# Two 1024 x 1024 branch products in seven half-size products each, their weight sums made in DRAM

## Chip, cores, metric

The kernel runs on one core of a Trainium2 chip. The metric is the device time of one execution in microseconds. Its five engines are TensorE (PE in the profile: matmuls, and weight loads as PEld), VectorE (DVE), ScalarE (ACT), GpSimd (POOL) and SyncE (SP, which here only issues transfers). Each works through its own list in order; semaphores order them against each other.

## What is computed

Two transformer blocks over 512 tokens of width 1024, all in float32. The change lies in the mixing part of the second block:

```python
a = gmlp_spatial_gating(z_u, z_v, ...)         # 512 x 1024
b = forgetting_attention(q, k, v, f_logit, b_f) # 512 x 1024
y_a = a @ w_branch_a                            # 1024 x 1024 weights
y_b = b @ w_branch_b
merged = gate_a * y_a + gate_b * y_b
x = x + merged @ w_out
```

## The kernel before

Activations lie transposed in SBUF: feature on the partition, eight tiles of 128 features by 512 tokens. A float32 product is made of three products of rounded parts: hi x hi, hi x lo and lo x hi. So each operand is split before use: ScalarE writes the high part (a copy into an fp32r tile), VectorE the low part (raw minus high). Weights come as strips of 1 MB (128 x 2048: 256 output features by the whole contraction). A strip has one of three slots: SyncE loads it into w_raw (line 590, after the slot's last product), ScalarE copies it to w_hi (L1375), VectorE writes w_lo over w_raw (L1951). The numbers of the phases (`PHASES`, `FIRST`) fix the order of all strips; `unit_done` counts two units a strip.

`stream` (with `feature_k`, L767 to L769) makes a plain product: 4 strips, 2 units each, a unit being 8 x 3 matmuls of 512 tokens into one PSUM bank, four banks in turn. Some feed-forward products are made instead in seven products of half size (`seven`, L1189 to L1191: Strassen's scheme in Winograd's form), there with tokens as output partitions and weights as the moving operand; their weight sums come from GpSimd's accumulating transfers (`part_sums`, L714) and VectorE.

The order around the change: attention 2a, woven with the product zv; the product u; the products qk2b and v2b; attention 2b woven with gate_b; gate_a; branch_b (operand: the attention, in att_t, split to b_hi and b_lo); branch_a (operand: the gated gMLP, in u_t, split to a_hi and a_lo); out2 (operand: merged); then the up product. VectorE multiplies branch_b's result into merged (L2626), branch_a's into gate_t (L2634), adds the two (L2636) and splits (L2638; ScalarE L1815). In out2 it adds to x (L2030). x waits in DRAM (x_kept) during attention 2b, whose buffers lie in its place, and is loaded back by SyncE (L613) at gate_a's last strip. In the attentions GpSimd stages operands (L667) and normalises score tiles (L674) that TensorE then transposes (L985); VectorE inverts the sums (L2105).

Of the kernel before, what the change touches and what calls it, by code (L numbers as in the profile page):

```python
# [13 lines left out]
P = 128  # L14
D = 1024
# [59 lines left out]
PHASES += [("branch_b", 4), ("branch_a", 4), ("out2", 4)]  # L75
# [9 lines left out]
STRIP_AT = {s: n for n, s in enumerate(s for s in range(N_STRIPS) if s not in MADE)}  # L85


def raw_count(s):

    return 16 * sum(n not in MADE and n not in SPARE for n in range(s, 0, -W_SLOTS))  # L90
# [4 lines left out]
FILLS = {name: 2 * n for name, n in PHASES} | {"wo_att": 8, "ple": 8} | {name: 2 * len(ADDED) for name in SEVEN}  # L95
# [67 lines left out]
def build(nc, d, out):  # L163
    ctx = ExitStack()
    with ctx:
# [139 lines left out]

        up_pad = [sb(f"up_pad{j}", [P, CONV2 - 1 + T], at=work + 2048 + 520 * j) for j in range(4)]
# [104 lines left out]
        m_hi = sem("m_hi")  # L411
        m_lo = sem("m_lo")
# [10 lines left out]
        amix_hi = sem("amix_hi")  # L423
        amix_lo = sem("amix_lo")
# [32 lines left out]
        pool_out_ready, POOL_OUT0 = seg_done, SPARE0 + 32 * len(SEVEN)  # L457

# [41 lines left out]
        def summed_count(g, i):  # L500

            return 16 * (4 * g + list(A_STAGE).index(i) + 1)

        def part_of(part, g):
            k, n = part
            return d["parts"][4 * g + 2 * n + k]

# [24 lines left out]
        def _(sp_eng):  # L532
# [50 lines left out]
            for s in range(1, N_STRIPS):  # L583
                j = s % W_SLOTS
                if s in MADE or s in SPARE:
                    continue
                if s >= W_SLOTS:

                    sp_eng.wait_ge(unit_done, 2 * (s - W_SLOTS) + 2)
                sp_eng.dma_start(w_raw[j].rearrange("p k n -> p (k n)"), d["strips"][STRIP_AT[s]]).then_inc(raw_loaded[j], 16)  # L590
                if s in PARTS_AT:
                    first_parts(PARTS_AT.index(s))
# [17 lines left out]
                if s == FIRST["gate_a"] + 3:  # L610

                    sp_eng.wait_ge(pv_done, 2 * 3 * HEADS8)
                    sp_eng.dma_start(x, x_kept).then_inc(x_loaded[0], 16)  # L613
# [12 lines left out]
        def _(pool):  # L626
# [23 lines left out]
            def attention(call, qk_phase):  # L650
# [37 lines left out]
                for n in range(TILES + 1):  # L688
                    if n and not causal:
                        normalize(n - 1)  # L690
                    if n < TILES - TT:
                        for part in ((0, 1), (2, 3, 4) if causal else (2, 3), (), ())[n % TT]:
                            stage(n // TT + 1, part)
                    if causal and n and n % 2 == 0:

                        normalize(n - 2)
                        normalize(n - 1)

# [9 lines left out]

# [17 lines left out]
            attention("2a", "qk2a")  # L726
            attention("2b", "qk2b")
            for g in range(FF_SEVEN, len(SEVEN)):
# [9 lines left out]
        def _(pe):  # L738
# [538 lines left out]
            stream("branch_b", feature_k, B, ready=lambda k: pe.wait_ge(att_lo, 4 + k + 1))  # L1277
            stream("branch_a", feature_k, A, ready=wait_tiles(amix_lo))
# [1626 lines left out]
```

## Time and profile before

| | |
|---|---|
| median of three runs | 1606.87 us (1606.82 to 1606.89) |
| the profiled execution | 1607.59 us |
| its span | 1605.9 us |
| TensorE busy | 1587.6 us, 99% |
| VectorE, ScalarE, GpSimd busy | 67%, 44%, 11% |
| branch_b starts, up product starts | 1052.45, about 1183 us |

The span runs from the first instruction to the last, the time has some 1.7 us more around it. A matmul's duration overlaps its neighbours', so the distance between starts is what one costs. In a group of instructions the columns are the count, busy time and mean ns of one, and the idle time of the engine before them with what ended it.

### The profile page before, as it was taken

Reading aid. Unit: us, or ns where it says so; the run is one execution under the profiler, and the core shown is the slowest. Engines: PE = TensorE matmul, PEld = TensorE weight load, DVE = VectorE, ACT = ScalarE, POOL = GpSimd, SP = SyncE. Lnnn points to the kernel's source line nnn. Section 1 sums busy time; section 2 is a strip of 40 time slices with the busy share of each in tenths; the row PEclk is TensorE's granted clock in tenths of the full one; section 3 lists DMA queues with packets and bytes.
Section 4 is the critical chain, followed back from the end, with each engine's and each line's share of the span. In section 5 each row is a group of like instructions: output and inputs, shape, how many; then the busy total and the mean of one; then the engine's idle time right before and its main releaser. Section 6 shows DMA issues by size and latency. Waiting matters only on the chain.

```text
span 1605.9 us, 20446 instructions
## 1 busy us (share of the span) xinstructions
PE 1587.6 (99%) x8187; PEld 1305.8 (81%) x8187; DVE 1078.5 (67%) x1494; ACT 710.6 (44%) x1018; POOL 181.5 (11%) x263
## 2 busy tenths in 40 slices
PE   9999999999999999999999999999999999999998
PEld 7877777888888888878788887888888888888888
DVE  6756788669393865657744477445566876878857
ACT  6524575545252524415662156342334443443544
POOL 0001055000000000024500255000000000000000
PEclk9999999999999999999999999999999999999999
DMA  5233321264757522331022211322237347344221
GB/s 191 80 106 125 123 95 53 79 210 131 236 132 235 131 106 94 116 138 72 27 105 83 101 53 53 136 101 105 93 143 262 102 135 238 93 154 158 105 106 53
DMA packets 32894, 195.14 MB, mean 122 GB/s; under 512 B 4320, under 2 KB 6816, under 8 KB 11296
## 3 DMA queue, kind: packets, MB, share of 16 engines
q1 hardware_dynamic: 25056, 160.20, 27.0%
q0 software_dynamic: 2880, 20.97, 6.8%
q10 hardware_dynamic: 4864, 12.66, 2.2%
q8 instruction: 65, 1.06, 0.3%
q14 instruction: 29, 0.24, 0.0%
HBM read 187.50 MB, written 6.32 MB: 121 GB/s over the span
## 4 chain that ended last, share of the span: by engine, by line
PE 87%; DVE 7%; issue 2%; ACT 2%; POOL 1%; DMA 0%; DVEq 0%; ACTq 0%; POOLq 0%
PE bank L767 20%; PE bank L769 19%; PE bank L768 19%; PE bank L1189 3%; PE bank L1190 3%; PE bank L1191 3%; PE bank L815 3%; PE bank L817 3%; PE bank L816 3%; PE bank L1000 1%; PE bank L775 1%; PE bank L985 1%; DVE w_lo L2370 1%; PE bank L744 1%; DVE up_c L2668 1%
## 5 line engine op out<-in xcount | busy, mean ns | idle before, releaser
L767 PE MATMUL bank<-a_hi,w_hi 128*128 128x512 f32 x1160 | 456.8, 394 | 0.6 <-DVE x L2030 0.6
L769 PE MATMUL bank<-a_hi,w_lo 128*128 128x512 f32 x1160 | 452.0, 390 | 0.0
L768 PE MATMUL bank<-a_lo,w_hi 128*128 128x512 f32 x1160 | 451.6, 389 | 0.0
L1375 ACT ACTIVATE w_hi<-w_raw 128x2048 fp32r<-128x2048 f32 x95 | 181.3, 1908 | 184.5 <-DMA w_raw<-in_strips 182.7
L769 PEld LDWEIGHTS bank<-a_hi,w_lo 128*128 128x128 f32 x1160 | 217.8, 188 | 45.9
L767 PEld LDWEIGHTS bank<-a_hi,w_hi 128*128 128x128 f32 x1160 | 217.9, 188 | 45.3 <-issue 2.3
L768 PEld LDWEIGHTS bank<-a_lo,w_hi 128*128 128x128 f32 x1160 | 218.0, 188 | 43.0 <-issue 0.2
L1951 DVE TENSOR_TENSOR w_lo<-w_raw,w_hi 128x2048 fp32r<-128x2048 f32 x92 | 210.9, 2293 | 54.4 <-ACT w_hi L1375 54.3
L1189 PE MATMUL bank<-w_hi,t_hi 128*128 128x512 f32 x280 | 109.3, 390 | 0.1
L1191 PE MATMUL bank<-w_hi,t_lo 128*128 128x512 f32 x280 | 109.0, 389 | 0.0
L1190 PE MATMUL bank<-w_lo,t_hi 128*128 128x512 f32 x280 | 109.0, 389 | 0.0
L767 PE MATMUL bank<-b_hi,w_hi 128*128 128x512 f32 x240 | 93.6, 390 | 0.4 <-DVE b_lo L2684 0.4
L768 PE MATMUL bank<-b_lo,w_hi 128*128 128x512 f32 x240 | 93.4, 389 | 0.0
L769 PE MATMUL bank<-b_hi,w_lo 128*128 128x512 f32 x240 | 93.4, 389 | 0.0
L815 PE MATMUL bank<-w_hi,a_hi 128*128 128x512 f32 x224 | 90.8, 405 | 0.0
L714 POOL DMA_DIRECT2D a_part<-in_parts x20 | 17.4, 868 | 643.6 <-DMA a_part<-in_parts 431.9
L816 PE MATMUL bank<-w_lo,a_hi 128*128 128x512 f32 x224 | 87.4, 390 | 0.0
L817 PE MATMUL bank<-w_hi,a_lo 128*128 128x512 f32 x224 | 87.4, 390 | 0.0
L1845 ACT ACTIVATE up_c<-up_pad,conv_w 128x512 f32<-128x512 f32 x44 | 35.8, 816 | 115.1 <-DVE up_pad L2022 115.1
L2668 DVE SCALAR_TENSOR_TENSOR up_c<-up_pad,conv_w,up_c 128x512 f32<-128x512 f32 x88 | 65.8, 747 | 1.8 <-ACT up_c L1845 0.3
L2370 DVE TENSOR_TENSOR w_lo<-a_part,w_hi 128x2048 fp32r<-128x2048 f32 x25 | 57.1, 2285 | 10.7 <-ACT w_hi L1664 10.7
L2022 DVE TENSOR_TENSOR up_pad<-bank,rstd 128x512 f32<-128x512 f32 x44 | 30.3, 691 | 49.4 <-PE bank L769 49.4
(364 smaller groups left out, 2658.0 us busy)
## 6 DMA issues: line engine op xcount, KB each, us to landing
w_raw<-in_strips SPq DMA_DIRECT2D x107, 1024.0 KB, 4.8
a_part<-in_parts SPq DMA_DIRECT2D x25, 1024.0 KB, 7.4
a_part<-in_parts POOLq DMA_DIRECT2D x20, 1024.0 KB, 9.1
spare<-in_parts SPq DMA_DIRECT2D x5, 1024.0 KB, 15.0
spare<-in_strips SPq DMA_DIRECT2D x5, 1024.0 KB, 4.9
seg_in<-cum_kept ACTq DMA_DIRECT2D x16, 256.0 KB, 3.5
x_kept<-x ACTq DMA_DIRECT2D x2, 2048.0 KB, 9.2
x<-x_kept SPq DMA_DIRECT2D x2, 2048.0 KB, 9.9
```

The costliest lines, as they stand in the source:

```text
L767: mm(ps[:, :], w_hi[slot][:, k, cols], hi[:, k, :], start=(k == 0), stop=False)
L768: mm(ps[:, :], w_hi[slot][:, k, cols], lo[:, k, :], start=False, stop=False)
L769: return mm(ps[:, :], w_lo[slot][:, k, cols], hi[:, k, :], start=False, stop=(k == kt - 1))
L815: mm(bank[j][:, :], hi[:, q, tok], w_hi4[slot][:, k, :], start=(q == 0), stop=False)
L816: mm(bank[j][:, :], hi[:, q, tok], w_lo4[slot][:, k, :], start=False, stop=False)
L817: return mm(bank[j][:, :], lo[:, q, tok], w_hi4[slot][:, k, :], start=False, stop=(q == KT - 1))
L1189: mm(ps[:, :], hi[:, k, tok], w_hi4[slot][:, k, :], start=(first and k == 0), stop=False)
L1190: mm(ps[:, :], hi[:, k, tok], w_lo4[slot][:, k, :], start=False, stop=False)
L1191: last = mm(ps[:, :], lo[:, k, tok], w_hi4[slot][:, k, :], start=False, stop=(end and k == W4 - 1))
L1375: run(w_hi[j], w_raw[j], ACT.Copy).then_inc(hi_split, 1)
L1951: v.tensor_tensor(w_lo[j], w_raw[j], w_hi[j].bitcast(F32), ALU.subtract).then_inc(strip_split, 1)
L2668: v.scalar_tensor_tensor(up_c[q], up_pad[q][:, j:j + T], flat[:, at * (CONV2 + 1) + j:at * (CONV2 + 1) + j + 1], up_c[q], ALU.mult, ALU.ad ...
```

## The change

Both branch products become seven products each of half size, by features: output features stay on the partitions, and each product has half of the contraction, half of the output features and half of the tokens. A product has two halves h (two banks), each with two blocks e of 128 features side by side in one bank, each 4 x 3 matmuls of 256 tokens. Some products accumulate on top of earlier ones in banks 4 to 7; ScalarE takes copies of the earlier states (`keep_first`, `keep_second`) before the bank goes on. Seven strips a branch take the place of four. Three of the seven weight operands are plain quarters of the weights, four are sums. The sums are made in a DRAM tensor `pre`: eight copies of 1 MB, DRAM to DRAM, on SyncE's queue behind the strip loads of ff2_3 and after; eight accumulating transfers on GpSimd's queue, four inside attention 2a (at n = 6, 10, 14, 18) and four during u. The strips of the seven come into two buffers in x's place, which are loaded in turn (`fold_at`), and x comes back in two halves with the first two strips of out2. The operand's quadrants are summed and split by VectorE and ScalarE in an order that is written out. out2 stays plain, but its first four units go by halves of the contraction, the first half of all four and then the second. In `PHASES` the branches have 7 strips; in `FILLS` 10 evacuations each.

```diff
-PHASES += [("branch_b", 4), ("branch_a", 4), ("out2", 4)]
+FOLD = ["branch_b", "branch_a"]
+QUADS = [(0, 0), (1, 0), (0, 1), (1, 1)]
+FOLD_BANK = [6, 4, 6, 4, 6, 0, 2]
+FOLD_QUAD = [1, 0, 1, 2, 3, 0, 2]
+FOLD_FOUR = {0: 1, 1: 0, 3: 2, 4: 3}
+FOLD_THREE = {2: 0, 5: 1, 6: 2}
+THREE_QUAD = [(1, 0), (0, 0), (0, 1)]
+THREE_RAW = [(0, 0), (1, 0), (0, 1)]
+MERGED_QUAD = [(0, 0), (1, 0), (1, 1), (0, 1)]
+FOLD_SOURCE = [0, (0, 0), 2, (1, 0), 3, 1, (1, 1)]
+PRE_SUMS = [(0, 1), (0, 0), (0, 0), (1, 0)]
+PRE_COPIES = [(kind, f) for kind in range(4) for f in range(2)]
+PHASES += [(name, 7) for name in FOLD] + [("out2", 4)]
...
+        FOLD_AT = [place["x"], place["x"]]
+        fold_raw = [[sb(f"fold_raw{f}_{j}", [P, KT, STRIP], at=FOLD_AT[f] + 2048 * j) for j in range(2)] for f in range(2)]
+        pre = nc.dram_tensor("pre", (4, 2, P, KT * STRIP), F32, kind="Internal").ap()
...
+        def quad(buf, i, j, h=None):
+            rows = slice(4 * j, 4 * j + 4) if h is None else slice(4 * j + 2 * h, 4 * j + 2 * h + 2)
+            return buf[:, rows, T // 2 * i:T // 2 * (i + 1)]
...
+                    n = s - FIRST[FOLD[0]]
+                    if n == 0:
+                        sp_eng.wait_ge(pv_done, 2 * 3 * HEADS8)
+                        sp_eng.wait_ge(summed, 16 * (8 + 4 * FF_SEVEN))
+                    elif n != 1:
+                        sp_eng.wait_ge(*low_ready(s - 2))
+                    f, i = FOLDED[s]
+                    source = FOLD_SOURCE[i]
+                    sp_eng.dma_start(flat(fold_at(s)), pre[source, f] if isinstance(source, int) else fold_part(f, source)).then_inc(fold_loaded[n % 3], 16)
+                    continue
...
+                    h = s - FIRST["out2"]
+                    half = slice(4 * h, 4 * h + 4)
+                    sp_eng.wait_ge(*low_ready(FIRST["out2"] - 2 + h))
+                    sp_eng.dma_start(x[:, half, :], x_kept[:, half, :]).then_inc(x_loaded[0], 16)
+                if 0 <= s - FIRST["ff2_3"] - 1 < len(PRE_COPIES):
+                    kind, f = PRE_COPIES[s - FIRST["ff2_3"] - 1]
+                    sp_eng.dma_start(pre[kind, f], fold_part(f, PRE_SUMS[kind])).then_inc(copied[kind // 2], 16)
                 if s in PARTS_AT:
                     first_parts(PARTS_AT.index(s))
...
+            def add_part(kind, f):
+                if f == 0:
+                    pool.wait_ge(summed, 16 * (4 * FF_SEVEN + (0, 0, 4, 6)[kind]))
+                if f == 0 and kind in (0, 2):
+                    pool.wait_ge(copied[kind // 2], COPIED0[kind // 2] + 16 * 4)
+                other = (fold_part(f, (1, 1)), fold_part(f, (0, 1)), pre[0, f], pre[2, f])[kind]
+                pool.dma_start(pre[kind, f], other, accum_op=ALU.add, max_dma_last_dim=8192).then_inc(summed, 16)
             def clear_stage1(parity):
...
             attention("2b", "qk2b")
             for g in range(FF_SEVEN, len(SEVEN)):
                 part_sums(g)
...
+            def fold_bank(f, i, h):
+                e0 = EVAC0[FOLD[f]]
+                if i in (2, 3):
+                    pe.wait_ge(snapped, SNAPPED0 + 4 * f + 2 * (i - 2) + h + 1)
+                elif i == 4:
+                    pe.wait_ge(dve_evac, e0 + h + 1)
+                elif f:
+                    pe.wait_ge(dve_evac, EVAC0[FOLD[f - 1]] + {0: 4, 1: 2, 5: 6, 6: 8}[i] + h + 1)
...
+            def folded(f):
+                for i in range(7):
+                    s = FIRST[FOLD[f]] + i
+                    slot, (t, k0) = s % W_SLOTS, QUADS[FOLD_QUAD[i]]
+                    hi, lo = quad(fold_hi[f], t, k0), quad(fold_lo[f], t, k0)
+                    pe.wait_ge(*low_ready(s))
+                    if i in FOLD_THREE:
+                        pe.wait_ge(three_lo, 3 * f + FOLD_THREE[i] + 1)
+                    else:
+                        pe.wait_ge(four_lo, 4 * f + FOLD_FOUR[i] + 1)
+                    for h in range(2):
+                        fold_bank(f, i, h)
+                        for e in range(2):
+                            ps = bank[FOLD_BANK[i] + h][:, e * (T // 2):(e + 1) * (T // 2)]
+                            cols = slice((2 * h + e) * P, (2 * h + e + 1) * P)
+                            for k in range(W4):
+                                mm(ps, w_hi4[slot][:, k, cols], hi[:, k, :], start=(e == 0 and k == 0 and i in (0, 1, 5, 6)), stop=False, skip_group_check=True)
+                                mm(ps, w_hi4[slot][:, k, cols], lo[:, k, :], start=False, stop=False, skip_group_check=True)
+                                last = mm(ps, w_lo4[slot][:, k, cols], hi[:, k, :], start=False, stop=(k == W4 - 1), skip_group_check=True)
+                        last.then_inc(unit_done, 1)
+            for f in range(len(FOLD)):
+                folded(f)
+            for half in range(2):
+                pe.wait_ge(four_lo, 4 * 2 + 2 * half + 2)
+                for j in range(4):
+                    if half == 0 and j % 2 == 0:
+                        pe.wait_ge(strip_split, FIRST["out2"] + j // 2 + 1)
+                    if half == 0:
+                        bank_free("out2", j)
+                    for k in range(4 * half, 4 * half + 4):
+                        last = feature_k(bank[j], (FIRST["out2"] + j // 2) % W_SLOTS, j % 2, B, k)
+                    if half:
+                        last.then_inc(unit_done, 1)
+            stream("out2", feature_k, B, begin=4)
...
+            def high_strip(f, i):
+                s = FIRST[FOLD[f]] + i
+                act.wait_ge(fold_loaded[(s - FIRST[FOLD[0]]) % 3], fold_count(s))
+                act.wait_ge(unit_done, 2 * (s - W_SLOTS) + 2)
+                run(w_hi[s % W_SLOTS], fold_at(s), ACT.Copy).then_inc(hi_split, 1)
...
+            def keep_first(f):
+                if f:
+                    act.wait_ge(dve_evac, EVAC0[FOLD[f - 1]] + 10)
+                for h in range(2):
+                    act.wait_ge(unit_done, 2 * FIRST[FOLD[f]] + h + 1)
...
+            high_four(0, 0)
+            high_four(0, 1)
+            hi(FIRST["gate_a"] + 3)
+            high_four(0, 2)
+            high_four(0, 3)
+            sigmoids("gate_a", gate_t, 0, 4)
+            high_strip(0, 0)
+            sigmoids("gate_a", gate_t, 4, 6)
+            high_strip(0, 1)
+            sigmoids("gate_a", gate_t, 6, KT)
             load_sqrt()
...
+            high_strip(0, 2)
+            high_four(1, 0)
+            high_four(1, 1)
+            keep_first(0)
+            high_three(0, 0)
+            high_strip(0, 3)
+            keep_second(0)
+            high_three(0, 1)
+            high_strip(0, 4)
+            high_strip(0, 5)
+            high_four(1, 2)
+            high_strip(0, 6)
...
+            high_three(1, 2)
+            high_merged(0)
+            high_merged(1)
+            hi(FIRST["out2"])
+            high_merged(2)
+            hi(FIRST["out2"] + 1)
+            high_merged(3)
...
+            def low_strip(f, i):
+                s = FIRST[FOLD[f]] + i
+                j = s % W_SLOTS
+                dve.wait_ge(hi_split, s)
+                v.tensor_tensor(w_lo[j], fold_at(s), w_hi[j].bitcast(F32), ALU.subtract).then_inc(strip_split, 1)
...
+            def low_four(f, n):
+                t, k = QUADS[n]
+                dve.wait_ge(four_hi, 4 * f + n + 1)
+                low = quad(fold_lo[f], t, k)
+                raw = quad(fold_three[f], t, k) if n == 1 else quad(fold_src[f], t, k)
+                v.tensor_tensor(low, raw, quad(fold_hi[f], t, k).bitcast(F32), ALU.subtract).then_inc(four_lo, 1)
...
+            def low_three(f, n):
+                dve.wait_ge(three_hi, 3 * f + n + 1)
+                low = quad(fold_lo[f], *THREE_QUAD[n])
+                v.tensor_tensor(low, quad(fold_src[f], *THREE_RAW[n]), quad(fold_hi[f], *THREE_QUAD[n]).bitcast(F32), ALU.subtract).then_inc(three_lo, 1)
...
+            def keep_sums(f):
+                src, e0 = fold_src[f], EVAC0[FOLD[f]]
+                dve.wait_ge(fold_sum, FOLD_SUM0 + 4 * f + 4)
+                for h in range(2):
+                    product_ready(f, 2, h)
+                    dve.wait_ge(snapped, SNAPPED0 + 4 * f + 2 + h + 1)
+                    v.tensor_tensor(quad(src, 0, 0, h), halves(6 + h), quad(fold_src[f], 1, 1, h), ALU.add).then_inc(dve_evac, 1)
...
+            def gate_part(f, i, j, ready):
+                new, gate, total = quad(fold_src[f], 1, 0), quad(gate3, i, j), quad(merged3, i, j)
+                if f == 0:
+                    fold_do(v.tensor_tensor(total, total, new, ALU.mult))
+                else:
+                    fold_do(v.tensor_tensor(new, new, gate, ALU.mult))
+                    v.tensor_tensor(total, total, new, ALU.add).then_inc(merged_ready, 1)
+                    dve.wait_ge(merged_ready, ready)
...
+            def take_21(f):
+                src, e0 = fold_src[f], EVAC0[FOLD[f]]
+                for h in range(2):
+                    product_ready(f, 4, h)
+                    v.tensor_tensor(quad(src, 1, 0, h), halves(6 + h), quad(src, 1, 1, h), ALU.add).then_inc(dve_evac, 1)
+                dve.wait_ge(dve_evac, e0 + 6)
+                gate_part(f, 1, 0, 2)
...
+            def take_22(f):
+                src, e0 = fold_src[f], EVAC0[FOLD[f]]
+                for h in range(2):
+                    product_ready(f, 5, h)
+                    v.tensor_tensor(quad(src, 1, 0, h), halves(h), quad(src, 0, 0, h), ALU.subtract).then_inc(dve_evac, 1)
+                for h in range(2):
+                    dve.wait_ge(dve_evac, e0 + 6 + h + 1)
+                    fold_do(v.tensor_tensor(fold_q[f][h], fold_q[f][h], quad(src, 1, 0, h), ALU.add))
+                gate_part(f, 1, 1, 3)
...
+            def take_12(f):
+                src, e0 = fold_src[f], EVAC0[FOLD[f]]
+                for h in range(2):
+                    product_ready(f, 6, h)
+                    v.tensor_tensor(quad(src, 1, 0, h), halves(2 + h), fold_q[f][h], ALU.add).then_inc(dve_evac, 1)
+                dve.wait_ge(dve_evac, e0 + 10)
+                gate_part(f, 0, 1, 4)
...
+            def fold_sums(f, n):
+                src, at = fold_src[f], FOLD_SUM0 + 4 * f
...
             for j in range(KT):
                 scaled_evac("gate_a", j, gate_t[:, j * T:(j + 1) * T])
...
+                if 1 <= j <= 4:
+                    low_four(0, j - 1)
+                if j in (4, 6):
+                    low_strip(0, j // 2 - 2)
+                if j in (0, 3, 5, 7):
+                    fold_sums(0, (0, 3, 5, 7).index(j))
...
+            low_four(1, 0)
+            fold_sums(1, 0)
+            low_strip(0, 2)
+            low_four(1, 1)
+            fold_sums(1, 1)
+            low_three(0, 0)
+            low_strip(0, 3)
+            fold_sums(1, 2)
+            low_three(0, 1)
+            low_strip(0, 4)
+            keep_sums(0)
+            low_strip(0, 5)
+            low_four(1, 2)
+            take_11(0)
+            low_strip(0, 6)
+            low_three(0, 2)
+            fold_sums(1, 3)
+            take_21(0)
+            low_four(1, 3)
+            low_strip(1, 0)
...
+            low_three(1, 2)
+            low_merged(0)
+            take_21(1)
+            low_merged(1)
+            lo(FIRST["out2"])
+            take_22(1)
+            low_merged(2)
+            lo(FIRST["out2"] + 1)
+            take_12(1)
+            low_merged(3)
+            dve.wait_ge(x_loaded[0], 64)
...
```

## Rows read from the trace of the kernel before

**Rows 1.** The page: busy time by engine, and the chain that ended last.
```profile
PE 1587.6 (99%) x8187; PEld 1305.8 (81%) x8187; DVE 1078.5 (67%) x1494; ACT 710.6 (44%) x1018; POOL 181.5 (11%) x263
...
PE 87%; DVE 7%; issue 2%; ACT 2%; POOL 1%; DMA 0%; DVEq 0%; ACTq 0%; POOLq 0%
```

**Rows 2.** Table of stretches: stretch, length; PE, PEld, DVE, ACT, POOL busy; granted clock; DMA.
```profile
1052.00:1096.00 44.00, 44.00 (x196) 36.44 (x195) 19.04 (x20) 14.58 (x17) 0.00 (x0) 1.00 0.26 96
```

**Rows 3.** Timeline of TensorE in the first up product and the gate product.
```profile
1219.76 0.39 PE L768 MATMUL bank<-a_lo,w_hi 128*128 128x512 f32 x1
...
1255.12 0.39 PE L768 MATMUL bank<-a_lo,w_hi 128*128 128x512 f32 x1
...
1574.76 0.28 PE L1326 MATMUL bank<-a_lo,w_hi 128*128 128x256 f32 x1
...
1583.88 0.28 PE L1327 MATMUL bank<-a_hi,w_lo 128*128 128x256 f32 x1
```

**Rows 4.** Groups of instructions, shapes apart, whole execution.
```profile
L1951 DVE TENSOR_TENSOR w_lo<-w_raw,w_hi 128x2048 fp32r<-128x2048 f32 x92 | 210.9, 2293 | 54.4 <-ACT w_hi L1375 54.3
...
L1375 ACT ACTIVATE w_hi<-w_raw 128x2048 fp32r<-128x2048 f32 x95 | 181.3, 1908 | 184.5 <-DMA w_raw<-in_strips 182.7 <-issue 1.7
...
L2392 DVE TENSOR_TENSOR t_lo<-t_raw,t_hi 128x1024 fp32r<-128x1024 f32 x25 | 30.4, 1216 | 0.0
...
L714 POOL DMA_DIRECT2D a_part<-in_parts x20 | 17.4, 868 | 643.6 <-DMA a_part<-in_parts 431.9 <-issue 211.6
...
L1676 ACT ACTIVATE t_hi<-hid 128x1024 fp32r<-128x1024 f32 x10 | 10.5, 1045 | 0.0
...
L2626 DVE TENSOR_TENSOR merged<-merged,bank 128x512 f32<-128x512 f32 x8 | 5.5, 686 | 24.5 <-PE bank L769 24.5
```

**Rows 5.** Timeline of PE, DVE and ACT around branch_b's start and in branch_a.
```profile
1052.45 0.39 PE L767 MATMUL bank<-b_hi,w_hi 128*128 128x512 f32 x1
...
1052.65 0.69 DVE L2022 TENSOR_TENSOR gate_t<-bank,rstd 128x512 f32<-128x512 f32 x1 [4.15 <-PE bank L769]
...
1054.03 1.28 ACT L1414 ACT_TABLE_LOAD   x1
...
1107.09 0.69 DVE L2636 TENSOR_TENSOR merged<-merged,gate_t 128x512 f32<-128x512 f32 x1
...
1107.82 0.63 ACT L1815 ACTIVATE b_hi<-merged 128x512 fp32r<-128x512 f32 x1 [15.77 <-DVE merged L2636]
...
1108.48 0.69 DVE L2638 TENSOR_TENSOR b_lo<-merged,b_hi 128x512 fp32r<-128x512 f32 x1 [0.70 <-ACT b_hi L1815]
1109.09 0.68 DVE L2634 TENSOR_TENSOR gate_t<-gate_t,bank 128x512 f32<-128x512 f32 x1
```

**Rows 6.** Transfers by issuer: count, KB each, median us from issue to landing.
```profile
w_raw<-in_strips SPq DMA_DIRECT2D x107, 1024.0 KB, 4.8
a_part<-in_parts SPq DMA_DIRECT2D x25, 1024.0 KB, 7.4
```

**Rows 7.** Timeline of GpSimd and TensorE in attention 2a, n = 8 to 11.
```profile
751.74 2.42 POOL L674 TENSOR_SCALAR score_2a<-score_2a,row_inv 128x384 f32<-128x384 f32 x2
...
754.03 0.27 PE L985 MATMUL bank<-ident,score_2a 128*128 128x128 f32 x1
...
756.95 1.35 POOL L674 TENSOR_SCALAR score_2a<-score_2a,row_inv 128x128 f32<-128x128 f32 x2 [0.37 <-DVE row_inv L2105]
...
758.16 0.27 PE L985 MATMUL bank<-ident,score_2a 128*128 128x128 f32 x1
```

**Rows 8.** Timeline of TensorE: the kernel's first matmuls and its last.
```profile
1.39 7.46 PE L1051 MATMUL bank<-b_lo 128*128 128x512 f32 x19 [1.39 <-POOL b_lo L628]
...
1599.73 1.16 PE L1338 MATMUL bank<-ident,norm_tok 128*128 128x128 f32 x8
```

**Rows 9.** Table of stretches behind the last matmul; columns as in rows 2.
```profile
1604.00:1604.90 0.90, 0.00 (x0) 0.00 (x0) 0.00 (x0) 0.00 (x0) 0.00 (x0) 1.00 0.99 340
1605.00:1605.90 0.90, 0.00 (x0) 0.00 (x0) 0.00 (x0) 0.00 (x0) 0.00 (x0) 0.50 0.03 8
```

More of the change, by code:

```diff
@@ L500, in summed_count @@
         def summed_count(g, i):
[L502 removed]
+            return 16 * (4 * g + (8 if SERIES[g] else 0) + list(A_STAGE).index(i) + 1)
         def part_of(part, g):
@@ L726, in _ @@
             attention("2a", "qk2a")
+            for n, (kind, f) in enumerate(PRE_COPIES[4:]):
+                pool.wait_ge(unit_done, 2 * (FIRST["u"] + n + 1))
+                add_part(kind, f)
             attention("2b", "qk2b")
@@ L1784, in _, with sigmoids @@
             attention("2b", "gate_b", None)
-            def sigmoids(phase, where):
-                for j in range(KT):
+            def sigmoids(phase, where, first, last):
+                for j in range(first, last):
                     act.wait_ge(dve_evac, EVAC0[phase] + j + 1)
@@ new lines, in high_four @@
+            def high_four(f, n):
+                t, k = QUADS[n]
+                src = quad(fold_src[f], t, k)
+                if n == 0 and f == 0:
+                    act.wait_ge(att_out, 3 * HEADS8)
+                elif n == 0 and f == 1:
+                    act.wait_ge(a_ready, KT)
+                    act.wait_ge(unit_done, 2 * FIRST["branch_b"])
+                elif n == 1:
+                    act.wait_ge(fold_sum, FOLD_SUM0 + 4 * f + 1)
+                    src = quad(fold_three[f], t, k)
+                run(quad(fold_hi[f], t, k), src, ACT.Copy).then_inc(four_hi, 1)
@@ new lines, in high_three, with halves, high_merged @@
+            def high_three(f, n):
+                act.wait_ge(fold_sum, FOLD_SUM0 + 4 * f + (3, 2, 4)[n])
+                act.wait_ge(unit_done, 2 * (FIRST[FOLD[f]] + (0, 1, 3)[n]) + 2)
+                run(quad(fold_hi[f], *THREE_QUAD[n]), quad(fold_src[f], *THREE_RAW[n]), ACT.Copy).then_inc(three_hi, 1)
+            def halves(b):
+                return bank[b][:, :].rearrange("p (e t) -> p e t", e=2)
+            def high_merged(n):
+                part = quad(by_tiles(merged), *MERGED_QUAD[n])
+                act.wait_ge(merged_ready, n + 1)
+                run(quad(b_hi, *MERGED_QUAD[n]), part, ACT.Copy).then_inc(four_hi, 1)
@@ new lines, in _ @@
+            low_three(0, 1)
[10 more added lines that the diff above has]
+            low_strip(1, 0)
+            take_22(0)
+            low_strip(1, 1)
+            take_12(0)
+            low_strip(1, 2)
+            low_three(1, 0)
+            low_strip(1, 3)
+            low_three(1, 1)
```

185 lines of the change are left out of this document (116 added, 69 removed).

## The prediction

> **What bounds the kernel now.** I read the page first: TensorE is busy for 99% of the span, and the chain that ended last is 87% TensorE [rows 1]. The table of stretches then says how tight the place of the change is: in the 44.0 us of the first branch product TensorE is busy for all 44.0, VectorE for 19.0, ScalarE for 14.6 [rows 2]; the stretches of the second branch and of the output product read the same, and the list of waits has no TensorE wait there. So time leaves only with matmul time, and any wait that the other engines put before a matmul is paid in full. The reader is to see both halves of that: matmuls are the only currency, and the two helpers have room on average, which says nothing about when they deliver.
>
> **Removed and added matmuls.** The durations in a group (390 ns) overlap, so the price is the distance from start to start in the timeline. Between 1219.76 and 1255.12 lie 156 matmuls with 512 columns: 226.7 ns each [rows 3]. The only long run with 256 columns is the final gate product: 76 of them between 1574.76 and 1583.88, 120.0 ns each; it has the same form as the new ones (a new 128x128 weight for each, features by 256 tokens). A branch has 4 strips x 2 units x 8 x 3 = 192 of the first kind, 43.5 us; in seven products 7 x 2 x 2 x 4 x 3 = 336 of the second kind, 40.3 us. That is 3.2 us a branch, **-6.4 us** for both, where counting columns alone would give 10.9. The output product keeps its 192 matmuls of 512.
>
> The Trainium skill (TensorE: Matmul & The Clock Gate, section Back-to-back issue gap) gives N/2.4 + 2.5 ns for the warm distance: 109.2 and 215.8 ns, so by the page, as an estimate, the saving would be 2 x (41.4 - 36.7) = 9.5 us. The rows have 120.0 and 226.7 for both, and the measurement decides.
>
> **Helper work, and where it is late.** The prices are in rows 4: VectorE 2.29 us for a strip's low part, 1.22 for a quadrant (1024 a row), 0.69 for half of one; ScalarE 1.91 and 1.05. Rows 5 show the joints: an instruction behind another starts 0.09 before that one's end (1108.48 + 0.69 against 1109.09), one that waits for another engine or for its own result 0.03 to 0.04 after (1107.78 against 1107.82). With these I laid out the new orders of ScalarE, VectorE, SyncE and TensorE from the end of the attention on. In both kernels the branch starts when the gate product ends, at 1052.45 [rows 5]; strips 0 and 1 and the first four quadrants are ready by then (low part of strip 1 at 1050). I write E0 for 1052.5.
>
> First late place, product 2 of branch_b. TensorE wants it at E0 + 4 x 2.88 = E0 + 11.5 = 1064.0. ScalarE has the last gate tile (ready 1053.3), its sigmoid, the table load and its one-element sqrt (1.3 + 0.2), the copy of strip 2 (1.9) and the high part of quadrant 0 of the gMLP operand (1.0): 1058.2. VectorE waits for that one, because low_four(1, 0) stands at the head of its list, and then goes 1.14 + 1.14 (fold_sums) + 2.20 (low part of strip 2) + 1.14 + 1.14 + 1.22 (low_three, which product 2 waits for) = 8.0: 1066.2 to 1066.3. **+2.3 us.** What is late next: nothing; snapshots and product 3's operands then come before TensorE asks, and the strips with them (two buffers, a load every 5.8 us).
>
> Second late place, the third unit of the output product. Write E for the end of product 6 of branch_a. Product 4 ends at E - 11.5. From 0.8 after it (the result's own delay, and low_merged(0) just ahead) VectorE runs take_21: 0.60 + 0.72 + 1.25 + 1.26 = 3.8; high_merged(1) 0.95 and the copy of strip out2+0, 1.95, on ScalarE; its low part 2.20; take_22: 2 x 0.60 + 2 x 0.72 + 1.25 + 1.26 = 5.15; high_merged(2) 0.95, the copy of strip out2+1 1.95, its low part 2.20; the first read of bank 2 in take_12, 0.73. Sum 19.9: E + 9.2. Units 0 and 1 with half of the contraction take 24 matmuls, 5.4 us, and are covered. Units 2 and 3 need that strip and banks 2 and 3, which product 6 used and take_12 empties last. Wait 9.2 - 5.4 = **+3.8 us**. The second half needs low_merged(3): 2 x 0.6 + 0.1 + 1.25 + 1.26 + 1.05 + 1.2 behind the strip's low part, E + 14.7, where TensorE arrives by itself at 14.7. Unit 4 waits 0.1 for its strip, since four units end together and VectorE has their additions. The tail into the up product is as before: the last addition hangs on the last unit. Each restart costs TensorE about 0.1: **+0.2**.
>
> **Moved transfers.** SyncE gets eight DRAM copies of 1 MB, one behind each of eight strip loads from ff2_3 on; a strip lands in 4.8 us and TensorE comes for it two strips (21.8 us) after its slot is free, so with 1.9 and 2.3 for the split some 12 us of delay cost nothing: 0. GpSimd gets eight accumulating issues. Four stand in the idle u stretch. Four stand in attention 2a, ahead of two normalisations each, and behind a normalisation wait transposes on TensorE. An issue of this queue takes 0.87 us [rows 4]. At n = 6 GpSimd has no idle time, so the pair of 2.42 us at 751.74 ends at 755.1 and its first about 0.7 before, at 754.3 (an estimate), against the transpose that started at 754.03; at n = 10 the pair at 756.95 had 0.37 of idle before it and starts at about 758.5, its first ends at 758.9 against 758.16 [rows 7]. Together **+0.7**; at n = 14 and 18 GpSimd idled over 1.6 us. Bounds: 0 if the slack of VectorE's inverse takes it, 4 x 0.9 = 3.6 if none is hidden. The nearest row for a DRAM to DRAM sum is this one into SBUF; I take it. The load of the kept x, 2 MB at gate_a's last strip, becomes two of 1 MB in the two strip loads of the output product; x is wanted at E + 17 and lands near E + 7: 0.
>
> The fold strips go through two buffers, so load, copy and low part (4.9 + 1.9 + 2.3 = 9.1) must fit in two products (11.5). They do with 4.8 us [rows 6]. Below 6 us of load I find +0.6 at most; at 7.4, the median of the part loads that share the queue [rows 6], about +7.
>
> **Sum.** -6.4 + 2.3 + 3.8 + 0.1 + 0.2 + 0.7 = **+0.7 us**. The profiled execution has a span of 1605.9 and a time of 1607.59, 0.7 over the median; 1605.9 becomes 1606.6, and the median 1606.87 becomes 1607.6.
>
> **Rivals.** (a) The waits don't appear and the matmuls decide: 1606.87 - 6.4 + 0.7 = 1601.2. For it: averages leave VectorE half idle [rows 2]. Against: each wait is a chain of round trips, not load. It decides once 3.9 of the 6.2 us of waits are missing, that is nearly always both. (b) Slower by the clock. At the end of the kernel the last matmuls start at 1599.73 and last 1.16; at 1604.0 to 1604.9 the granted clock is still 1.00, from 1605.0 on 0.50 (1.2 GHz), so it fell about 4 us after the last matmul [rows 8, 9]. My second wait is 3.8 us. If the clock falls in it, the start of the kernel prices the return: 19 matmuls of 512 columns took 7.46 us where 19 x 0.227 = 4.3 would do [rows 8], +3.1: 1610.7 (the column of granted clock reads 1.00 there as well, the distances don't). It decides from a wait of about 4 us on. (c) Loads slow down with the second hot buffer pair, +7: 1614. (d) The four issues in attention 2a are hidden nowhere: +2.9 more, 1610.5.
>
> The rule behind (b) is in the Trainium skill (TensorE: Matmul & The Clock Gate, section HAM oscillation): idle gaps between bursts bring half rate back. By that rule the trace's end agrees.
>
> **How the numbers follow.** The measurement can tell about 0.2%, 3.2 us. Forecast and its neighbours (either wait off by 1 us or so) 0.57, own range 1605.0 to 1610.0; (a) 0.16; (b) 0.11; (c) 0.07; (d) 0.09, half of it inside 0.2%. Faster: most of (a), 0.15. Slower: (b), (c), half of (d) and a tail of the forecast, 0.24. The range from 1602.0 to 1611.0 leaves out the far part of (a) and (c).
>
> **What would show it.** After: two branches of 672 matmuls with 256 columns at 120 ns; TensorE waits for low_three's line near E0 + 11.5 for about 2.3 us and for VectorE's reads of banks 2 and 3 in the output product for about 3.8; granted clock 1.00 throughout; a few tenths more of waiting for score_2a. The prediction is wrong if fold loads take over 6 us, if the distance at 256 columns is not 120 ns, or if other products wait too.

## The result, and the profile after

The changed kernel takes **1613.17 us** (median of 5 runs, 1612.71 to 1614.63) against 1606.87 before: ratio 1.0040, 95% interval 1.0026 to 1.0054. It is slower by 6.3 us. The forecast was 1607.6 and the range ended at 1611.0: wrong. The profiled execution has a span of 1612.0 (before: 1605.9) and a time of 1614.03, so 0.3 us of its difference lie around the span.

The page of the changed kernel, busy time and chain, answers [rows 1]:

```profile
PE 1587.1 (98%) x8475; PEld 1318.2 (82%) x8475; DVE 1118.0 (69%) x1512; ACT 730.5 (45%) x1026; POOL 186.5 (12%) x271
...
PE 83%; DVE 9%; ACT 3%; issue 2%; DMA 2%; POOL 1%; SPq 0%; DVEq 0%; ACTq 0%; POOLq 0%
```

TensorE is busy as long as before, though it has 6.4 us less to do: some of its matmuls must have become longer. The list of TensorE's waits names the new ones (total, times, longest):

```profile
PE bank L861 <- DVE u_t L2914: 3.8, 1, 3.8
...
PE bank L1405 <- issue: 2.2, 1, 2.2
PE bank L1079 <- POOL score_2a L754: 1.6, 2, 1.4
```

The first two are the late places of the prediction, in their predicted sizes (2.3 and 3.8). The third was 0.7 before. VectorE around the first of them, and then TensorE's timeline there, product 2 of branch_b:

```profile
1060.10 1.23 DVE L2835 TENSOR_TENSOR a_lo<-u_t,a_hi 128x1024 fp32r<-128x1024 f32 x1 [3.83 <-ACT a_hi L1953]
...
1066.86 1.22 DVE L2841 TENSOR_TENSOR b_lo<-att_t,b_hi 128x1024 fp32r<-128x1024 f32 x1
```

```profile
1065.64 0.28 PE L1407 MATMUL bank<-b_hi,w_lo 128*128 128x256 f32 x1
1068.17 0.55 PE L1405 MATMUL bank<-b_hi,w_hi 128*128 128x256 f32 x1 [2.25 <-issue]
1068.52 0.41 PE L1406 MATMUL bank<-b_lo,w_hi 128*128 128x256 f32 x1
...
1071.30 0.37 PE L1407 MATMUL bank<-b_hi,w_lo 128*128 128x256 f32 x1
1071.50 0.28 PE L1405 MATMUL bank<-b_hi,w_hi 128*128 128x256 f32 x1
```

VectorE stands still for 3.83 us until ScalarE has the high part of quadrant 0, and the operand of product 2 (low_three, L2841) is ready at 1068.08, 0.09 before TensorE goes on. That is the chain of the prediction, 1.8 us later because the branch starts 1.8 later. The list names "issue" there; the timelines show the operand. At the second, the third unit of out2:

```profile
1144.05 0.39 PE L863 MATMUL bank<-b_hi,w_lo 128*128 128x512 f32 x1
1148.25 0.77 PE L861 MATMUL bank<-b_hi,w_hi 128*128 128x512 f32 x1 [3.81 <-DVE u_t L2914]
1148.82 0.63 PE L862 MATMUL bank<-b_lo,w_hi 128*128 128x512 f32 x1
...
1153.08 0.55 PE L863 MATMUL bank<-b_hi,w_lo 128*128 128x512 f32 x1
1153.46 0.40 PE L861 MATMUL bank<-b_hi,w_hi 128*128 128x512 f32 x1
```

The reader is to see what stands behind the waits. From 1068.17 to 1071.50 there are 15 matmuls, 222 ns apart where 120 is the rule; from 1148.25 to 1153.46 there are 12, 434 ns apart where 227 is [rows 3]. The stretches (length; PE, PEld, DVE, ACT, POOL busy; granted clock; DMA share; GB/s) say why:

```profile
1054.00:1098.00 44.00, 41.75 (x334) 41.51 (x333) 36.78 (x32) 23.99 (x21) 0.00 (x0) 0.96 0.45 163
774.00:776.00 2.00, 0.90 (x4) 0.40 (x3) 2.00 (x5) 0.32 (x1) 0.17 (x1) 1.00 0.96 254
776.00:778.00 2.00, 1.31 (x6) 0.85 (x6) 1.94 (x5) 1.21 (x4) 1.76 (x3) 0.98 1.03 225
778.00:780.00 2.00, 1.84 (x9) 1.66 (x9) 2.00 (x6) 0.68 (x4) 0.61 (x1) 0.50 0.95 197
...
1066.00:1068.00 2.00, 0.00 (x0) 0.00 (x0) 2.00 (x3) 2.00 (x3) 0.00 (x0) 1.00 0.89 344
1068.00:1071.00 3.00, 2.83 (x13) 2.86 (x14) 3.00 (x3) 2.71 (x3) 0.00 (x0) 0.51 0.24 101
...
1145.00:1147.00 2.00, 0.00 (x0) 0.00 (x0) 1.79 (x1) 0.18 (x1) 0.00 (x0) 0.89 0.00 0
1147.00:1149.00 2.00, 0.75 (x2) 0.68 (x3) 1.97 (x4) 0.00 (x0) 0.00 (x0) 0.50 0.00 0
```

The granted clock fell to 0.50 (1.2 GHz) three times: at the end of the first wait, in the middle of the second, and at 778 in attention 2a, 1.6 us after matmuls had begun again behind the 1.4 us of waiting for score_2a. The first row answers [rows 2]: VectorE now has 36.8 us of work in 44 where it had 19.0.

Where the 6.1 us between the spans come from, by the first matmul of each part:

| part | before | after | difference |
|---|---|---|---|
| up to branch_b | 1052.45 | 1054.25 | +1.8 |
| both branches | 87.0 | 84.6 | -2.5 = -6.4 matmuls, +2.4 wait, +1.5 half clock |
| out2 | 43.5 | 50.3 | +6.8 = 4.0 wait, 2.5 half clock, 0.3 other |
| up product to the end | 422.9 | 422.9 | 0.0 |

(The wait is counted from where the next matmul was due; the half clock is 15 matmuls in 3.33 us less 1.80, and 12 in 5.21 less 2.72.) Before branch_b no matmul is new, so the 1.8 us are put down to the moved transfers, which the experiments then test. ScalarE and GpSimd of the changed kernel in attention 2a, and the transfers from 757 to 770:

```profile
768.54 1.06 ACT L1526 ACTIVATE w_hi<-w_raw 128x1024 fp32r<-128x1024 f32 x1 [0.72 <-DMA w_raw<-in_strips]
...
775.83 1.41 POOL L754 TENSOR_SCALAR score_2a<-score_2a,row_inv 128x128 f32<-128x128 f32 x2 [3.03 <-DVE row_inv L2320]
776.32 0.30 PE L1079 MATMUL bank<-ident,score_2a 128*128 128x128 f32 x1 [1.42 <-POOL score_2a L754]
```

```profile
pre<-in_parts POOLq DMA_DIRECT2D x2, 1024.0 KB, 9.8
w_raw<-in_strips SPq DMA_DIRECT2D x1, 1024.0 KB, 10.3
```

A strip that lands in 4.8 us otherwise [rows 6] takes 10.3 beside two accumulating transfers. ScalarE's copy of it, at the head of its list, starts at 768.54, before the change at 767.52; from there the same microsecond runs through VectorE and GpSimd (L754, 775.83 against 774.85) to the transposes (776.32 against 775.27). Then the clock falls, and 1.05 becomes 2.4, of which 0.6 is regained later. Against the forecast's span of 1606.6 the 5.4 us too many are thus: 4.0 of half clock behind the two waits, 1.1 more than the 0.7 of the moved transfers, 0.2 of waits and 0.1 of the rest.

### The profile page after: what moved, and what is told of

Read it like the earlier page. It is cut to its first block, busy times and chain, and to the rows that moved or that the text cites. A ratio compares the mean times of both kernels' runs of the same rounds, so it can differ in the third digit from the quotient of the medians.

```text
span 1612.0 us, 21100 instructions
## 1 busy us (share of the span) xinstructions
PE 1587.1 (98%) x8475; PEld 1318.2 (82%) x8475; DVE 1118.0 (69%) x1512; ACT 730.5 (45%) x1026; POOL 186.5 (12%) x271
## 4 chain that ended last, share of the span: by engine, by line
PE 83%; DVE 9%; ACT 3%; issue 2%; DMA 2%; POOL 1%; SPq 0%; DVEq 0%; ACTq 0%; POOLq 0%
PE bank L861 18%; PE bank L863 17%; PE bank L862 17%; PE bank L1283 3%; PE bank L1285 3%; PE bank L1284 3%; PE bank L909 3%; PE bank L911 3%; PE bank L910 3%; PE bank L1405 1%; PE bank L1406 1%; DMA w_raw<-in_strips 1%; PE bank L1407 1%; PE bank L1094 1%; PE bank L1079 1%
## 5 line engine op out<-in xcount | busy, mean ns | idle before, releaser
L861 PE MATMUL bank<-a_hi,w_hi 128*128 128x512 f32 x1096 | 431.9, 394 | 0.6 <-DVE x L2245 0.6
L863 PE MATMUL bank<-a_hi,w_lo 128*128 128x512 f32 x1096 | 427.1, 390 | 0.0
L862 PE MATMUL bank<-a_lo,w_hi 128*128 128x512 f32 x1096 | 426.7, 389 | 0.0
L863 PEld LDWEIGHTS bank<-a_hi,w_lo 128*128 128x128 f32 x1096 | 205.7, 188 | 43.4
L861 PEld LDWEIGHTS bank<-a_hi,w_hi 128*128 128x128 f32 x1096 | 205.9, 188 | 42.8 <-issue 2.3
L1520 ACT ACTIVATE w_hi<-w_raw 128x2048 fp32r<-128x2048 f32 x87 | 166.0, 1908 | 144.3 <-DMA w_raw<-in_strips 142.5
L2166 DVE TENSOR_TENSOR w_lo<-w_raw,w_hi 128x2048 fp32r<-128x2048 f32 x84 | 192.6, 2294 | 55.5 <-ACT w_hi L1520 55.4
L861 PE MATMUL bank<-b_hi,w_hi 128*128 128x512 f32 x176 | 70.0, 397 | 4.2 <-DVE u_t L2914 3.8
L862 PE MATMUL bank<-b_lo,w_hi 128*128 128x512 f32 x176 | 69.5, 395 | 0.0
L863 PE MATMUL bank<-b_hi,w_lo 128*128 128x512 f32 x176 | 69.4, 394 | 0.0
```

Of the source, the lines that this page charges most:

```text
L861: mm(ps[:, :], w_hi[slot][:, k, cols], hi[:, k, :], start=(k == 0), stop=False)
L862: mm(ps[:, :], w_hi[slot][:, k, cols], lo[:, k, :], start=False, stop=False)
L863: return mm(ps[:, :], w_lo[slot][:, k, cols], hi[:, k, :], start=False, stop=(k == kt - 1))
L1520: run(w_hi[j], w_raw[j], ACT.Copy).then_inc(hi_split, 1)
L2166: v.tensor_tensor(w_lo[j], w_raw[j], w_hi[j].bitcast(F32), ALU.subtract).then_inc(strip_split, 1)
```

## Experiments

Each was timed in five rounds beside the kernel before, whose median was 1607.3 in the first two series and 1607.1 in the third. Differences from the changed kernel are taken from its 1613.17; measured again in the third series (the last experiment) it has 1612.57, and every such difference is then 0.6 us smaller.

Each execution also has its mean granted clock on record, which helps where no profile was taken. The profiles without a fall of the clock before the end read 0.999 or 1.000, those with one fall 0.998 or 0.999, those with two and three 0.996 and 0.995. The kernel before reads 0.999 or 1.000 in all but 3 of the 64 executions that took under 1609 us beside these runs, and 0.998 in those three, so 0.998 is a strong sign of a fall but no proof; less it never read there.

**Fill the waits.** 18 and 16 matmuls whose results nobody reads (into banks 0 and 7), ahead of the two waits:

```diff
+WARM = (18, 16)
...
+                    if (f, i) == (0, 2) and WARM[0]:
+                        pe.wait_ge(dve_evac, EVAC0["gate_a"] + 5)
+                        for _ in range(WARM[0]):
+                            mm(bank[0][:, 0:T // 2], w_hi4[slot][:, 0, 0:P], w_hi4[slot][:, 0, 0:T // 2], start=True, stop=True)
...
+                    if half == 0 and j == 2:
+                        warm = w_hi4[FIRST["out2"] % W_SLOTS]
+                        for _ in range(WARM[1]):
+                            mm(bank[7][:, :], warm[:, 0, 0:P], warm[:, 0, :], start=True, stop=True)
```

> The changed kernel with extra matmuls that nobody reads in its two waits: 18 of 256 columns before product 2 of branch_b (bank 0, 2.2 us), 16 of 512 columns before the third unit of out2 (bank 7, 3.6 us). Theory C (the clock falls in the waits and its return is paid after them): the waits shrink to a few tenths, the matmuls behind them stand 120 and 227 ns apart at once, and the kernel gains 1.4 + 2.7 us: 1609.1. Rival W (a wait costs its own length only, and what looks like slow matmuls is paid anyway): extra matmuls in a wait change nothing, 1613.2.

Measured: 1608.96 us (1608.17 to 1610.10, 11 runs), ratio 1.0012 (1.0003 to 1.0021). 4.2 us come back (3.6 against the second measurement), though the useful matmuls still wait for the same operands, and the profile grants 1.00 at both places. The mean granted clock is 0.999 or 1.000 in all eleven executions, where the twelve of the changed kernel have 0.995 to 0.998. Theory C holds: the half clock behind the waits is a cost of its own.

**All eight additions after attention 2a.**

```diff
-                    if call == "2a" and n % TT == 2 and 1 <= n // TT <= 4:
-                        add_part(*PRE_COPIES[n // TT - 1])
...
-            for n, (kind, f) in enumerate(PRE_COPIES[4:]):
-                pool.wait_ge(unit_done, 2 * (FIRST["u"] + n + 1))
+            for n, (kind, f) in enumerate(PRE_COPIES):
+                pool.wait_ge(unit_done, 2 * (FIRST["u"] + n - 1))
```

> The changed kernel with all eight accumulating transfers after attention 2a, one a unit from the end of zv on. Theory A (the four in attention 2a cost the 1.8 us by which branch_b starts later: 1054.03 against 1052.22): branch_b starts at 1052.2 again, 1611.4. Rival B (the eight transfers cost wherever they stand, since 1 MB takes 9.5 us there and strips need the same engines): the delay moves into u or qk2b, 1613.2 or more.

Measured: 1610.86 us, ratio 1.0022 (1.0013 to 1.0031); 2.3 less than the changed kernel (1.7 against the second measurement), so A rather than B. From 735 us to branch_b nothing shifts against the kernel before. The single runs are the surprise: 1607.74 to 1612.75. The profiled one is the 1607.74, and it has both waits in full. TensorE's timeline there:

```profile
1065.72 0.36 PE L1403 MATMUL bank<-b_hi,w_hi 128*128 128x256 f32 x1 [2.26 <-issue]
1065.92 0.28 PE L1404 MATMUL bank<-b_lo,w_hi 128*128 128x256 f32 x1
1066.04 0.28 PE L1405 MATMUL bank<-b_hi,w_lo 128*128 128x256 f32 x1
...
1144.36 0.47 PE L859 MATMUL bank<-b_hi,w_hi 128*128 128x512 f32 x1 [3.82 <-DVE u_t L2912]
1144.67 0.39 PE L860 MATMUL bank<-b_lo,w_hi 128*128 128x512 f32 x1
1144.90 0.40 PE L861 MATMUL bank<-b_hi,w_lo 128*128 128x512 f32 x1
```

Same waits, no fall of the clock, distances of 120 and 230 ns at once. From the start of branch_b to the up product it takes 131.1 us, 130.6 in the kernel before, where the forecast's terms for this part add up to 0.0: without a fall the sum is right to 0.6 us. That its time is so near to the forecast's 1607.6 is in part luck, since the 0.7 us of the transfers don't arise here. Of the other ten executions seven have a mean granted clock of 0.997, one 0.996 and two 0.998, against 0.999 in this one: the clock fell in nearly all of them.

**A sixteenth of the data, all of the issues.** In attention 2a only 128 of 2048 columns are added; the rest of those sums is left out.

```diff
-                pool.dma_start(pre[kind, f], other, accum_op=ALU.add, max_dma_last_dim=8192).then_inc(summed, 16)
+                cols = slice(0, 128 if kind < 2 else KT * STRIP)
+                pool.dma_start(pre[kind, f][:, cols], other[:, cols], accum_op=ALU.add, max_dma_last_dim=8192).then_inc(summed, 16)
```

> The changed kernel with the four transfers of attention 2a cut to 128 of their 2048 columns, so that their sums are left out for the rest; their issues stay. Theory L (the strip load beside them takes 9.3 instead of 4.8 us, ScalarE's copy at the head of its list waits for it, and the delay runs through VectorE and GpSimd to TensorE, where the clock falls as well): only the issues' 0.3 us stay of 1.8, 1611.6. Rival P (the issues themselves, 0.83 us each on GpSimd): 1613.2 as before the cut. If both halves matter, about 1612.4.

Measured: 1611.34 us, ratio 1.0023 (1.0014 to 1.0032), near L's 1611.6; against the second measurement of the changed kernel the gain is 1.2, so the medians alone don't rule out P, and the trace has to decide. The strip lands in 4.9 us, and ScalarE's copy doesn't wait:

```profile
767.61 1.04 ACT L1527 ACTIVATE w_hi<-w_raw 128x1024 fp32r<-128x1024 f32 x1
...
1145.02 0.47 PE L862 MATMUL bank<-b_hi,w_hi 128*128 128x512 f32 x1 [3.82 <-DVE u_t L2915]
1145.33 0.39 PE L863 MATMUL bank<-b_lo,w_hi 128*128 128x512 f32 x1
...
1146.48 0.58 PE L862 MATMUL bank<-b_hi,w_hi 128*128 128x512 f32 x1
1146.86 0.63 PE L863 MATMUL bank<-b_lo,w_hi 128*128 128x512 f32 x1
```

In the profile branch_b starts no later than before. The last rows show a third form of the same wait: the clock fell 1.5 us after work had begun again. In this execution the first wait, 2.25 us, passed without a fall.

**Another order of the two helpers' lists.** What TensorE asks for next goes first:

```diff
-            low_four(1, 0)
             fold_sums(1, 0)
             low_strip(0, 2)
+            low_four(1, 0)
+            low_three(0, 0)
             low_four(1, 1)
-            fold_sums(1, 1)
-            low_three(0, 0)
             low_strip(0, 3)
+            fold_sums(1, 1)
...
+            take_22(1, rest=False)
             low_merged(1)
             lo(FIRST["out2"])
-            take_22(1)
-            low_merged(2)
+            gate_part(1, 1, 1, 3)
             lo(FIRST["out2"] + 1)
             take_12(1)
+            low_merged(2)
...
-            high_merged(2)
             hi(FIRST["out2"] + 1)
+            high_merged(2)
```

> The changed kernel with VectorE's and ScalarE's lists in another order: behind the gate product fold_sums, low part of strip 2, low_four, low_three; before the output product the bank reads of take_22 first, its product with the gate between the two strips' low parts, low_merged(2) last, and ScalarE's copy of the second strip ahead of high_merged(2). Laid out by hand, neither wait is left. Theory C (waits plus return of the clock): two branches take 80.7 instead of 84.8 us, out2 43.7 instead of 50.3: -10.6, 1602.6. Rival W (waits alone): -6.3, 1606.9. Rival M (other waits take their place): over 1608.

Measured: 1603.30 us, ratio 0.9976 (0.9967 to 0.9986); in the profile the branches take 80.7 us and out2 44.0, against 80.7 and 43.7 in C. Both waits are gone from the list; of TensorE's longer waits only that of attention 2a is new against before:

```profile
PE bank L1079 <- POOL score_2a L754: 1.6, 2, 1.4
```

9.9 us less than the changed kernel (9.3 against the second measurement), of which the waits' own length is 6.3: again C. Here the 1.4 us of waiting in attention 2a left the clock at 1.00. The two slowest of the nine executions (1604.56 and 1604.80) have a mean granted clock of 0.998, the others 0.999 or 1.000, so it may have fallen there in those.

**Both.**

> The changed kernel with the other order of VectorE's and ScalarE's lists and with all eight accumulating transfers after attention 2a. Theory (three causes that add up: the two waits with the clock's return, and the transfers in attention 2a): only the matmuls' saving is left, 1606.9 - 6.4 + 0.1 = 1600.6, and single runs lie as close together as those of the kernel before (about 2 us between lowest and highest). Rival (the causes overlap, one delay hides behind another): 1602 to 1603, no better than the orders alone.

Measured: 1601.67 us (1601.48 to 1603.04), ratio 0.9969 (0.9957 to 0.9981), the fastest of all. The median lies between the theory's 1600.6 and the rival's 1602 to 1603 and decides neither; against the kernel before the spans differ by 1605.9 - 1599.5 = 6.4, the medians by 5.6. Its stretch answers [rows 2]:

```profile
1052.00:1096.00 44.00, 44.00 (x368) 43.96 (x368) 40.32 (x35) 26.13 (x23) 0.00 (x0) 1.00 0.45 165
```

368 matmuls in 44.0 us (119.6 ns each), without a gap, while VectorE has 40.3 us of work: the branch has reached the point where VectorE is nearly as full as TensorE.

**One wait at a time, and half of each.** The kernel with the additions after attention 2a, once with the second part of the new order only (first wait left), once with the first only (second wait left), once with neither and 9 + 8 unread matmuls.

> The changed kernel with all eight accumulating transfers after attention 2a and the output product's part of the other order: only the wait before product 2 of branch_b (2.3 us) is left. Without any fall of the clock 1600.6 + 2.3 = 1602.9, with a fall 1.4 us more, 1604.3. Theory S (whether the clock falls in one and the same wait differs from execution to execution): single runs in two heaps 1.4 us apart. Rival F (it falls always or never in a wait of a given length): one heap.

Measured: 1604.32 us. Single runs: six from 1603.71 to 1604.32, three from 1605.08 to 1605.29, two at 1606.3. The profiled one (1604.25) has a wait of 2.3 us and a clock of 1.00. Heaps rather as S has them than as F, but three in place of two, 1.3 and 2.4 us above the lowest. The mean granted clock bears S out in part: 0.999 or 1.000 in the six low ones, 0.998 in three of the five others. The third heap stays unexplained; single runs of the kernel before lie 1.6 us apart as well.

> The changed kernel with all eight accumulating transfers after attention 2a and the first branch's part of the other order: only the wait before the third unit of out2 (3.8 us) is left. Without any fall of the clock 1600.6 + 3.8 = 1604.4, with a fall up to 2.7 us more, 1607.1. Theory S (differs from execution to execution): single runs spread between 1604.4 and 1607.1. Rival F (always in a wait of this length): all near 1607.

Measured: 1606.99 us, single runs 1606.40 to 1609.11, the profiled one with a wait of 3.81 and a clock of 0.50 behind it. Here F does better: none of eleven came out at 1604.4, and ten of them have a mean granted clock of 0.998 or less, so in the long wait the clock nearly always fell.

> The changed kernel with all eight accumulating transfers after attention 2a and 9 + 8 extra matmuls that nobody reads, which fill the first half of each wait: idle stretches of about 1.2 and 2.0 us stay in place of 2.3 and 3.8. Theory D (whether the clock falls depends on how long TensorE stands still): mostly no fall, 1607.7 with single runs close together, since the waits' ends stay where they were. Rival E (it falls whenever the work stops for a moment of this order): as with the full waits, 1610.9 with single runs over 5 us apart.

Measured: 1608.56 us (1607.68 to 1610.01). The profiled execution (1607.72) has waits of 1.1 and 2.0 us and a clock of 1.00. Between D and E, nearer to D: half the wait left as idle time costs under a third of the clock's price (0.9 of the 3.2 us between 1607.7 and 1610.9), while the ends of the waits stay where they were. But the single runs aren't close together, and four of the five slowest have a mean granted clock of 0.998 or less, the others 0.999 or 1.000: even with waits this short it fell in some executions.

**The transfers alone, in the kernel before.** Eight copies and eight additions of strips, into a tensor that nobody reads:

```diff
+                if 0 <= s - FIRST["ff2_3"] - 1 < len(PRE_COPIES):
+                    kind, f = PRE_COPIES[s - FIRST["ff2_3"] - 1]
+                    sp_eng.dma_start(pre[kind, f], d["strips"][8 * f + kind]).then_inc(copied[kind // 2], 16)
...
+                    if call == "2a" and n % TT == 2 and 1 <= n // TT <= 4:
+                        add_part(*PRE_COPIES[n // TT - 1])
```

> The kernel before with the change's transfers alone: the eight DRAM copies on SyncE's queue and the eight accumulating transfers on GpSimd's, four in attention 2a, on strips of the weights and into a DRAM tensor that nobody reads. Theory A (they are one of the causes and add up with the others: 1613.2 - 1610.9 = 2.3 between the changed kernel and the one with these four moved): 1607.3 + 2.3 = 1609.6, branch_b starts 0.6 to 1.9 us later, and single runs lie further apart than before, since the clock falls there in some. Rival (they hurt only together with the rest of the change): 1607.3.

Measured: 1608.40 us, ratio 1.0009 (0.9999 to 1.0018): +1.3, not 2.3, and at the edge of what can be told from nothing. The mechanism is there (strip in 9.9 us, ScalarE's wait for it, transposes 0.6 later, branch_b 0.7 later); no fall of the clock in this profile, nor a sign of one in the mean granted clock of the others (0.999 or 1.000).

**The changed kernel again.**

> The changed kernel once more, with more executions and another profiled one. Theory S (the waits are the same in each execution, whether the clock falls in them is not): 1612 to 1614 as median, the two waits of 2.3 and 3.8 us to 0.1 in the profile, but the stretches at half rate at other places or fewer, and single runs over 3 us apart. Rival F (all of it is fixed): the same three stretches, single runs within 2 us.

Measured: 1612.57 us (1610.97 to 1612.84, 7 runs). The waits are 2.3 and 3.8 once more, but this execution has two falls in place of three. Its stretches (length; PE busy; granted clock; DMA share; GB/s):

```profile
778.00:780.00 2.00, 2.00 (x16) 1.00 1.00 209
...
1066.00:1068.00 2.00, 1.10 (x5) 0.67 0.78 328
1068.00:1070.00 2.00, 2.00 (x11) 0.50 0.08 16
...
1148.00:1150.00 2.00, 2.00 (x6) 0.50 0.00 0
```

In attention 2a the clock holds, and branch_b starts 0.5 us late instead of 1.8. So the stretches are as S has them; the spread of the single runs, 1.9 us, is F's number. In all seven the mean granted clock is 0.996 to 0.998.

## Why the prediction was wrong

**The matmuls: right.** -6.4 us; the version without waits has it in its span.

**The two late places: right in place, cause and size.** 2.25 and 3.81 us for 2.3 and 3.8. That both fall away by the order alone, with the same work, shows them to be order and not load, as the argument against (a) had it.

**The clock: the step that failed.** The prediction had the mechanism as rival (b), but wrote that "it decides from a wait of about 4 us on", and left it out of the sum. That came from one observation, the kernel's end, where the clock held for about 4 us behind the last matmul [rows 8, 9]. One execution's delay was taken for a threshold, though nothing in it said that the next would be alike. The same place in the other profiles has it between 2.5 us (all additions after attention 2a: last matmul over at 1600.8, clock down at 1603.3) and 4.5 us (the transfers alone: 1601.6 and 1606.1). The profiles of the runs: of five waits of 2.25 us it fell in two, of five of 3.8 us in four, one of them 1.5 us after the restart; with 2.0 us once not, with 1.4 us once and once not, with 1.0 or 1.1 us in these places in none of four. What it costs is 1.5 us behind the first wait and 2.5 behind the second in the changed kernel's profile; over the medians 4.2 (or 3.6) by filling both waits. So the term that the sum had at 0 measured 4.0 us, most of the 5.4 by which the span was missed. Rival (b) priced +3.1 for one fall; single ones cost 1.5 and 2.5 here and 1.3 in attention 2a (of which 0.6 was regained later), and there are up to three places.

The Trainium skill (TensorE: Matmul & The Clock Gate, section What's actually happening) says that the gate's timing isn't tied to the kernel, so the point of change differs from run to run. The runs agree: the same 3.8 us wait had three outcomes in five executions (no fall once, a fall within the wait or at its end three times, one 1.5 us after it once). That rule, beside (b), spoke for a chance and not for a threshold.

**The moved transfers: right in sign, wrong in mechanism.** +0.7 was worked out from GpSimd's issues (0.83 us each). Counted from 735 us on, branch_b is 0.2 us late with a sixteenth of the data and all of the issues; with all of it 0.6 to 1.3 without a fall of the clock, 1.9 with one. By medians the transfers cost 1.3 (alone in the kernel before), 1.6 (1603.30 - 1601.67) or 2.3 (1613.17 - 1610.86; 1.7 against the second measurement). The delay is a strip load's, 10.3 in place of 4.8 us. The prediction granted the strips some 12 us of slack; in attention 2a there is slack for TensorE's need of the strip, but not for ScalarE, whose copy stands in its list ahead of the attention's own work. The rows to see it were there: the part loads that share the engines take 7.4 us [rows 6], which was priced for the fold strips and not for this strip. Rival (c) itself fell: the fold strips land in 4.8 us, as taken. The Trainium skill (DMA: Bandwidth & Descriptors, section SWDGE vs HWDGE vs iDMA) says that SyncE's and GpSimd's transfers go through the same engines, which take turns between them; 10.3 beside two of 9.8 agrees.

**What stays open.** The parts don't add up exactly: 2.65 for the first wait and 5.3 for the second, each alone, against 9.2 for both (1610.86 - 1601.67). Whether falls are more frequent when there are two waits, these runs can't say. That the upper heaps of single runs are executions with a fall is argued from their distance and, for most, from the mean granted clock; where in these executions it fell isn't on record. That the fall at 778 came of the 1.4 us wait before it is likely and not shown.

## What to carry to other kernels

Where TensorE sets the end, price a wait of a microsecond and a half or more as its length plus a chance of a stretch at half clock behind it, and compare versions by medians over many executions, not by one profile. Before accepting a wait, look at what stands ahead of the late operation in the helper's list; here another order of the same work gave 9 to 10 us, where filling the waits gave about 4. A transfer that is moved is to be checked against each load that runs beside it, and the load against the first instruction that waits for it, not the last.

## What was not expected of the hardware

- The clock can fall while matmuls already run again: 1.5 us after the restart behind a wait of 3.8 us. The same wait left it at 1.00 in another execution (1607.74 us, where the median of that version is 1610.86).
- In one execution the clock fell 1.6 us after the end of a wait of 1.42 us among short matmuls (0.50 from 778 to 780), and in another with the same 1.42 there it didn't.
- An addition of 1 MB from DRAM to DRAM takes 9.5 to 9.8 us, twice a strip load, and doubles a load that runs beside it.
